# State visits of a hybrid decoder step: the outer product of dt·x and B made on VectorE from PSUM instead of on GpSimd from a copy

## The chip, the cores and the metric

One Trainium2 chip, one of its cores. The time is that of one launch of the whole program in device microseconds, the median of several runs. A profiled execution of the same program gives the span and the rows below.

## What is computed

One inference step of a layer with two branches, for a prompt of 512 tokens and a decode batch of 8 samples. The part that the change touches is the sample side of the state-space branch. For each of 8 samples b, 32 heads of 64 rows and 128 state columns:

```
h' = exp(dt*A) * h + (dt*x) outer B        # new state, an output
y  = C . h'                                # read of the state
```

The kernel treats the 32·64 = 2,048 rows as 16 units u of 128 partitions; a unit is a tile of 128 partitions x 8 samples x 128 columns (512 KB), loaded from the input and stored to the output. Four units share a group g of B and C. y is not read from the new state: the kernel forms C.h from the old state, scales it by the decay, and adds (dt*x)*(B.C) afterwards. So the new state is only stored, and the old one is read before it is overwritten.

## The kernel before

The kernel is written by hand for each engine. One list, PLAN, gives the order of steps; each engine walks it and issues its part of each step, so every engine's queue is in program order and semaphores join them. Projections are float32 products split in a high and a low part (three products each): each weight item is loaded by SyncE (`w_raw`), rounded to `wH` by ScalarE (L1136, a helper for all its copies) and its rest `wL` made by VectorE (L1511, both inputs in SBUF). TensorE takes PSUM banks 0 to 3 in turn for the projections and waits for VectorE's or ScalarE's `free` of the unit two before.

The 16 visits are laid beside 19 pieces of projection work, "beats" 0 to 18: three gs pieces (0 to 2), four ga (3 to 6), four ba (7 to 10), four ga (11 to 14), four ba (15 to 18). A gs or ga piece is 48 matmuls of 260 columns, a ba piece 24. In a beat the order is: the next item's `wH` and `wL` where one is due, TensorE's piece, at beats 4, 8 and 12 the spreads of a new group (`sgroup`), the visit (`sread`), ScalarE's decay of the visit before (`sdecay`), SyncE's load of a later unit into a freed slot (`sload`), and the use of the piece's result; a ba piece's use adds to `mix` on VectorE (L1622) and frees its two banks. From beat 14 on ScalarE and VectorE also split the prompt's y into `yH` and `yL` (L1925, both inputs in SBUF), four units a beat.

For a group, `sgroup` makes TensorE spread the samples' C row over all partitions into banks 4 and 5 and the B row into banks 6 and 7 (L920). ScalarE's `sbcopy` copies banks 6 and 7 to `Bsp` in SBUF and frees them at once. A visit is then:

- VectorE: `sc` = slot times the C spread in banks 4 and 5 (L1898, two halves), and a reduction of `sc` to y8 (L1905). After the fourth visit's `sc` it frees banks 4 and 5, ahead of the reduction.
- ScalarE: the decay of the slot, 8 instructions (L1429), once `sc` has been read.
- GpSimd: `outer` = Bsp times XD (dt·x) (L1116), then slot + outer (L1121), then the store's issue (L1123).

There are five slots; SyncE reloads one (L1001) once its store has landed, and its queue also holds the weight loads and the shifts of the key/value caches.

Of the kernel before, what the change touches and what calls it, by code (L numbers as in the profile page):

```python
# [21 lines left out]
ALU = mybir.AluOpType  # L22
ACT = mybir.ActivationFunctionType
AX = mybir.AxisListType

P = 128
D = 1024
T = 512
B = 8
# [7 lines left out]
UNITS = DSSD // P  # L37
PER_GROUP = UNITS // GROUPS
# [56 lines left out]
def plan():  # L95
# [128 lines left out]
    for beat, (kind, j, unit) in enumerate(rest):  # L224
        use = proj(kind, j, unit=unit)
        if beat < UNITS:
            if beat and beat % PER_GROUP == 0:
                out.append(("sgroup", beat // PER_GROUP))
            out.append(("sread", beat))
        if beat % PER_GROUP == 1 and beat < UNITS:  # L230
            out.append(("sbcopy", beat // PER_GROUP))
        if 0 < beat <= UNITS:
            out.append(("sdecay", beat - 1))
        if SLOTS_S <= beat - 2 < UNITS:
            out.append(("sload", beat - 2))
        if kind == "ba" and j == 1 and unit > 0:
            out.append(("sfinal", unit - 1))
        out.append(use)
        left = len(rest) - 1 - beat
        if left <= 4:  # L240
            out += [("parts", u) for u in range(4 * (4 - left), 4 * (5 - left)) if u < UNITS]
# [77 lines left out]
def hybrid_kernel(nc, xT, wpack, params, consts, sel_in, state_conv, ssm_in, caches,  # L319
                  y_out, tail_out, ssmp_out, kvp_out, ssms_out, kvs_out):  # L320
    ctx = ExitStack()
    with ctx:
# [3 lines left out]
        def sb(name, shape, dt=F32):  # L326
# [136 lines left out]
        Bsp = a4.tile("Bsp", [P, B, P])  # L463
        outer = a4.tile("outer", [P, B, P])
# [19 lines left out]
        names = """squares_added ac_parts_ready act_order b_rows_ready b_spread_ready b_spread_used bc_samples_kept cache_shifted cached_v_used  # L484
# [10 lines left out]
            sample_dt_ready sample_exponents sample_exps sample_probs sample_probs_turned  # L495
# [534 lines left out]
        def _(pool):  # L1030
            nbar = 0
            outs = 0
            for step in PLAN:
# [75 lines left out]
                elif op == "sread":  # L1109
# [3 lines left out]
                    pool.wait_ge(S["b_spread_ready"], 2 * (g + 1))  # L1113
                    if u == 0:
                        pool.wait_ge(S["sample_xdt_ready"], 1)
                    nc.gpsimd.tensor_tensor(outer[:, :, :], Bsp[:, :, :], XD[:, u, :].unsqueeze(2).to_broadcast([P, B, P]),  # L1116
                                            ALU.mult).then_inc(S["sample_outer_ready"], 1)
# [3 lines left out]
                    nc.gpsimd.tensor_tensor(st_u[:, :, :], st_u[:, :, :], outer[:, :, :], ALU.add).then_inc(S["sample_state_ready"], 1)  # L1121
# [8 lines left out]
        def _(act):  # L1130
# [4 lines left out]
            def cp(out, in_):  # L1135
                return nc.scalar.copy(out, in_)  # L1136

            def free(bk):
                act.sem_inc(bk.freed, 1)
# [10 lines left out]
            for step in PLAN:  # L1150
# [261 lines left out]
                elif op == "sbcopy":  # L1412

                    g = a[0]
                    if g > 0:
                        act.wait_ge(S["sample_outer_ready"], PER_GROUP * g)
                    for half in range(2):
                        bk = banks[6 + half]
                        bk.full(act, ("Bsp", g, half))
                        cp(Bsp[:, 4 * half:4 * half + 4, :], bk.tile[:, :].rearrange("p (c n) -> p c n", c=4)).then_inc(S["b_spread_ready"], 1)  # L1420
                        act.wait_ge(S["b_spread_ready"], 2 * g + half + 1)
                        free(bk)
# [25 lines left out]
        def _(dve):  # L1448
# [5 lines left out]
            def free(bk):  # L1454
                dve.sem_inc(bk.freed, 1)  # L1455
# [4 lines left out]
            for step in PLAN:  # L1460
# [428 lines left out]
                elif op == "sread":  # L1889
# [11 lines left out]
                    dve.wait_ge(S["sample_state_read"], u + 1)  # L1901
                    if u % PER_GROUP == PER_GROUP - 1:
                        free(banks[4])
                        free(banks[5])
                    ch.link(V.tensor_reduce(y8[:, u, :], sc[:, :, :], AX.X, ALU.add))  # L1905
# [138 lines left out]
```

## Time and profile before

| what | us |
|---|---|
| median of 3 runs | 1186.77 (1186.63 to 1190.5) |
| the profiled execution's own time | 1187.57 |
| its span | 1185.8 |

The profiled execution is 0.8 us above the median, and 1.8 us of its time lie outside the span. The visits run from about 917 us (first `sc`) to 1029 us (last store's issue) of the span; TensorE is busy almost throughout, with a few gaps that the rows below give, and from 1042 us it works on the last projections.

### The profile page before, as it was taken

The numbers are of one execution on the slowest core, as the hardware profiler recorded it, in microseconds if no ns is written. First come the engines' busy times: TensorE is split into PE (matmuls) and PEld (weight loads), VectorE is DVE, ScalarE is ACT, GpSimd is POOL, SyncE is SP. The second block draws the span as 40 slices with busy tenths as digits, with TensorE's granted clock in tenths as the row PEclk, the third lists the DMA queues.
The fourth block names the chain that finished last, engine by engine and source line by source line (L and its number), as shares of the span: only waits on it lengthen the run. The fifth ranks groups of instructions, "written<-read, shape, count | busy, mean of one in ns | idle before, by whom it ended". The sixth has DMA issues, their size and how long they took to land.

```text
span 1185.8 us, 19650 instructions
## 1 busy us (share of the span) xinstructions
PE 1097.8 (93%) x7838; PEld 1010.2 (85%) x7838; DVE 656.7 (55%) x936; ACT 499.4 (42%) x1130; POOL 219.8 (19%) x209
## 2 busy tenths in 40 slices
PE   4999989999999989895999999999998999689998
PEld 3887779977988779775999899898998999689998
DVE  6663527622462347237677677776764466834342
ACT  5334533345333544102554645656445566612210
POOL 0330003400231000000211220221120589500000
PEclk9998899989999899756999999999999999789999
DMA  8546102580242047145056246254446899432221
GB/s 348 213 169 276 55 1 116 213 329 1 107 168 81 1 151 246 58 152 232 1 219 235 109 162 254 110 218 163 182 175 273 343 360 343 155 144 80 100 98 46
DMA packets 29819, 198.14 MB, mean 167 GB/s; under 512 B 4104, under 2 KB 6280, under 8 KB 20224
## 3 DMA queue, kind: packets, MB, share of 16 engines
q1 hardware_dynamic: 25712, 183.35, 40.5%
q0 software_dynamic: 4016, 13.54, 3.0%
q8 instruction: 62, 1.02, 0.3%
q14 instruction: 29, 0.24, 0.1%
HBM read 180.16 MB, written 104.70 MB: 240 GB/s over the span
## 4 chain that ended last, share of the span: by engine, by line
PE 73%; DVE 11%; ACT 7%; issue 4%; DMA 2%; POOL 2%; SPq 0%; DVEq 0%; ACTq 0%; POOLq 0%
PE bank L618 36%; PE bank L590 16%; DVE cacc L1575 2%; PE bank L813 2%; PE bank L715 2%; ACT wH L1136 2%; PE bank L678 2%; PE bank L767 2%; POOL t L1080 2%; PE bank L884 1%; PE bank L654 1%; DVE wL L1511 1%; DMA slot<-in_state_ssm 1%; PE bank L902 1%; PE bank L876 1%
## 5 line engine op out<-in xcount | busy, mean ns | idle before, releaser
L1511 DVE TENSOR_TENSOR wL<-w_raw,wH 128x2048 fp32r<-128x2048 f32 (+1 forms) x63 | 145.0, 2302 | 155.0 <-ACT wH L1136 152.9
L618 PE MATMUL bank<-xH,wH 128*128 128x260 f32 x976 | 207.9, 294 | 8.1 <-DVEq L1455 6.9
L618 PE MATMUL bank<-xH,wL 128*128 128x260 f32 x976 | 198.1, 285 | 0.0
L618 PE MATMUL bank<-xL,wH 128*128 128x260 f32 x976 | 197.8, 284 | 0.0
L1136 ACT CAST wH<-w_raw 128x2048 fp32r<-128x2048 f32 (+1 forms) x63 | 119.2, 1892 | 136.2 <-PE bank L618 84.8
L618 PEld LDWEIGHTS bank<-xH,wH 128*128 128x128 f32 x976 | 152.0, 191 | 18.8 <-issue 16.6
L618 PEld LDWEIGHTS bank<-xH,wL 128*128 128x128 f32 x976 | 152.0, 190 | 0.0
L618 PEld LDWEIGHTS bank<-xL,wH 128*128 128x128 f32 x976 | 152.0, 190 | 0.0
L590 PE MATMUL bank<-wH,xH 128*128 128x512 f32 x336 | 136.7, 407 | 10.0 <-DVE xL L1490 6.0
L590 PE MATMUL bank<-wH,xL 128*128 128x512 f32 x336 | 134.6, 401 | 0.0
L590 PE MATMUL bank<-wL,xH 128*128 128x512 f32 x336 | 134.6, 401 | 0.0
L590 PEld LDWEIGHTS bank<-wH,xH 128*128 128x128 f32 x336 | 84.0, 250 | 21.2 <-issue 7.0
L1080 POOL TENSOR_TENSOR t<-qn,ropeB 128x256 f32<-128x256 f32 (+1 forms) x60 | 56.0, 951 | 246.4 <-DVE qn L1539 246.3
L590 PEld LDWEIGHTS bank<-wL,xH 128*128 128x128 f32 x336 | 84.1, 250 | 7.8
L590 PEld LDWEIGHTS bank<-wH,xL 128*128 128x128 f32 x336 | 84.3, 251 | 7.4
L1575 DVE SCALAR_TENSOR_TENSOR cacc<-buf,wcv,cacc 128x544 f32<-128x544 f32 x72 | 56.5, 784 | 17.3 <-ACT cacc L1251 15.1
L1294 ACT ACTIVATE Sx<-Sx,nm 128x128 f32<-128x128 f32 x96 | 37.6, 392 | 57.9 <-DVE nm L1669 57.8
L1381 ACT ACTIVATE Lb<-bank,nac 128x128 f32<-128x128 f32 x128 | 36.7, 369 | 47.1 <-PE bank L862 44.3
L1104 POOL TENSOR_TENSOR Eb<-Eb,CT 128x512 f32<-128x512 f32 x32 | 54.0, 1707 | 11.7 <-ACT Eb L1372 11.7
L618 PE MATMUL bank<-yH,wH 128*128 128x260 f32 x256 | 52.6, 287 | 3.5 <-DVE yL L1928 3.5
L618 PE MATMUL bank<-yL,wH 128*128 128x260 f32 x256 | 52.5, 287 | 0.0
L618 PE MATMUL bank<-yH,wL 128*128 128x260 f32 x256 | 52.2, 285 | 0.0
(285 smaller groups left out, 1916.9 us busy)
## 6 DMA issues: line engine op xcount, KB each, us to landing
w_raw<-in_weights SPq DMA_DIRECT2D x62, 1024.0 KB, 5.3
out_kvs<-in_cache SPq DMA_DIRECT2D x16, 2044.0 KB, 10.2
ring<-in_cache SPq DMA_DIRECT2D x48, 256.0 KB, 3.2
slot<-in_state_ssm SPq DMA_DIRECT2D x16, 512.0 KB, 5.9
out_ssm_s<-slot POOLq DMA_DIRECT2D x16, 512.0 KB, 6.0
out_kvs<-in_cache SPq DMA_DIRECT2D x8, 508.0 KB, 8.8
out_kvp<-st POOLq DMA_DIRECT2D x9, 256.0 KB, 2.3
out_kvp<-vv POOLq DMA_DIRECT2D x9, 256.0 KB, 4.6
```

Source lines behind the costliest of these rows:

```text
L590: mm = pe.matmul(bk.tile[:, :], a[:, kk, cols], wslot(b, i)[:, k, :], start=(kk == 0 and n == 0), stop=(kk == KD - 1 and n == 2))
L618: mm = pe.matmul(bk[hf].tile[:, 0:HALF], wslot(w, i)[:, k, s * P:(s + 1) * P], x[:, k, hf * HALF:(hf + 1) * HALF], start=(k == 0 and n == ...
L678: mm = pe.matmul(bk.tile[:, t * P:(t + 1) * P], qT[o:o + HD, hp, t * P:(t + 1) * P], kT[o:o + HD, hp, t * P:(t + 1) * P], start=True, stop ...
L715: mm = pe.matmul(out, vv[:, t, h * HD:(h + 1) * HD], PT[:, n % 2, t, :], start=(t == 0), stop=True, skip_group_check=True)
L767: mm = pe.matmul(banks[6].tile[:, c:c + B + 1:B], KT[:, n % 2, hp, :], qd[:, q0, :], start=True, stop=True, skip_group_check=True)
L1080: ins = nc.gpsimd.tensor_tensor(o[:, :, x, :], v[:, :, 1 - x, :], rb, ALU.mult)
L1104: nc.gpsimd.tensor_tensor(Eb[:, u % 2, e, :], Eb[:, u % 2, e, :], CT[:, 0:T], ALU.mult).then_inc(S["scaled_c_ready"], 1)
L1136: return nc.scalar.copy(out, in_)
L1294: ins = A(Sx[:, n % 2, t, :], Sx[:, n % 2, t, :], ACT.Exp, bias=nm[:, n % 2, t:t + 1], accum_out=lst[:, g, t, h:h + 1])
L1381: ins = A(Lb[:, e, c, :], banks[5 + e].tile[:, c * P:(c + 1) * P], ACT.Exp, bias=nac[:, c, n:n + 1])
L1511: TT(wL[:, i % 2, 0:k * n], raw[:, i % 2, 0:k * n], wH[:, i % 2, 0:k * n].bitcast(F32), ALU.subtract)\
L1575: ins = STT(out=cacc[:, :], in0=bb[:, w:w + CONV], scalar=wcv[:, cu, w:w + 1], in1=cacc[:, :], op0=ALU.mult, op1=ALU.add)
```

## The change

VectorE makes `outer` itself, straight from banks 6 and 7, between a visit's `sc` and its reduction. `outer` has two buffers in place of `Bsp` and one; ScalarE's copy and GpSimd's product are gone. VectorE waits, before it overwrites an `outer` buffer, for GpSimd's addition two visits before. All four spread banks are now freed at a group's fourth visit, after its reduction. `sample_xdt_ready` is still signalled; nobody waits for it.

```diff
-        if beat % PER_GROUP == 1 and beat < UNITS:
-            out.append(("sbcopy", beat // PER_GROUP))
...
-        Bsp = a4.tile("Bsp", [P, B, P])
-        outer = a4.tile("outer", [P, B, P])
+        outer = a4.tile("outer", [P, 2, B, P])
...
-                    pool.wait_ge(S["b_spread_ready"], 2 * (g + 1))
-                    if u == 0:
-                        pool.wait_ge(S["sample_xdt_ready"], 1)
-                    nc.gpsimd.tensor_tensor(outer[:, :, :], Bsp[:, :, :], XD[:, u, :].unsqueeze(2).to_broadcast([P, B, P]),
-                                            ALU.mult).then_inc(S["sample_outer_ready"], 1)
                     pool.wait_ge(S["sample_outer_ready"], u + 1)
                     pool.wait_ge(S["sample_decayed"], u + 1)
                     st_u = slots[u % SLOTS_S]
-                    nc.gpsimd.tensor_tensor(st_u[:, :, :], st_u[:, :, :], outer[:, :, :], ALU.add).then_inc(S["sample_state_ready"], 1)
+                    nc.gpsimd.tensor_tensor(st_u[:, :, :], st_u[:, :, :], outer[:, u % 2, :, :], ALU.add).then_inc(S["sample_state_ready"], 1)
...
-                elif op == "sbcopy":
-
-                    g = a[0]
-                    if g > 0:
-                        act.wait_ge(S["sample_outer_ready"], PER_GROUP * g)
-                    for half in range(2):
-                        bk = banks[6 + half]
-                        bk.full(act, ("Bsp", g, half))
-                        cp(Bsp[:, 4 * half:4 * half + 4, :], bk.tile[:, :].rearrange("p (c n) -> p c n", c=4)).then_inc(S["b_spread_ready"], 1)
-                        act.wait_ge(S["b_spread_ready"], 2 * g + half + 1)
-                        free(bk)
...
                     ins.then_inc(S["sample_state_read"], 1)
                     dve.wait_ge(S["sample_state_read"], u + 1)
+                    if u >= 2:
+                        dve.wait_ge(S["sample_state_ready"], u - 1)
+                    for half in range(2):
+                        bk = banks[6 + half]
+                        bk.full(dve, ("Bsp", g, half))
+                        ins = TT(outer[:, u % 2, 4 * half:4 * half + 4, :], bk.tile[:, :].rearrange("p (c n) -> p c n", c=4),
+                                 XD[:, u, 4 * half:4 * half + 4].unsqueeze(2).to_broadcast([P, 4, P]), ALU.mult)
+                    ins.then_inc(S["sample_outer_ready"], 1)
+                    ch.link(V.tensor_reduce(y8[:, u, :], sc[:, :, :], AX.X, ALU.add))
                     if u % PER_GROUP == PER_GROUP - 1:
-                        free(banks[4])
-                        free(banks[5])
-                    ch.link(V.tensor_reduce(y8[:, u, :], sc[:, :, :], AX.X, ALU.add))
+                        dve.wait_ge(S["sample_outer_ready"], u + 1)
+                        for bk in banks[4:8]:
+                            free(bk)
```

VectorE's queue at visit 7, the last of group 1, before (slot_158 is its slot, filled4 and filled5 are the C spread's banks):

```order
L1511 TENSOR_TENSOR wL<-w_raw,wH 128x2048 [waits s_weight_high_ready,s_dve_order]
L1898 TENSOR_TENSOR sc<-slot_158,bank 128x512 [waits filled4,s_state_loaded2]
L1898 TENSOR_TENSOR sc<-slot_158,bank 128x512 [waits filled5]
L1905 TENSOR_REDUCE y_164<-sc 128x8 [waits s_sample_state_read]
L1622 SCALAR_TENSOR_TENSOR mix<-mix,bank 128x260 [waits filled2,s_gate_ready,s_dve_order]
L1622 SCALAR_TENSOR_TENSOR mix<-mix,bank 128x260 [waits s_dve_order,filled3]
```

and the same place with the change (names and lines are numbered one or more lower there):

```order
L1492 TENSOR_TENSOR wL<-w_raw,wH 128x2048 [waits s_weight_high_ready,s_dve_order]
L1879 TENSOR_TENSOR sc<-slot_157,bank 128x512 [waits filled4,s_state_loaded2]
L1879 TENSOR_TENSOR sc<-slot_157,bank 128x512 [waits filled5]
L1888 TENSOR_TENSOR outer<-bank,XD 128x512 [waits filled6,s_sample_state_ready,s_sample_state_read]
L1888 TENSOR_TENSOR outer<-bank,XD 128x512 [waits filled7]
L1891 TENSOR_REDUCE y_163<-sc 128x8
L1603 SCALAR_TENSOR_TENSOR mix<-mix,bank 128x260 [waits s_dve_order,s_sample_outer_ready,filled2,s_gate_ready]
L1603 SCALAR_TENSOR_TENSOR mix<-mix,bank 128x260 [waits s_dve_order,filled3]
```

Two products stand between `sc` and the reduction, and the group's banks, freed before the reduction, are now freed behind it.

The other place is ScalarE's queue at the start of group 2, before:

```order
L1429 ACTIVATE slot_158<-slot_158,dsb 128x128 [waits s_sample_state_read]
L1429 ACTIVATE slot_158<-slot_158,dsb 128x128 x7
L1136 COPY Bsp<-bank 128x512 [waits filled6,s_sample_outer_ready]
L1136 COPY Bsp<-bank 128x512 [waits s_b_spread_ready,filled7]
L1429 ACTIVATE slot_159<-slot_159,dsb 128x128 [waits s_b_spread_ready,s_sample_state_read]
```

With the change the two copies are gone there, and the decay of visit 8 stands directly behind that of visit 7.

## Rows read from the trace of the kernel before

**Rows 1.** The page: engine, busy us, share of the span, instructions.
```profile
PE 1097.8 (93%) x7838; PEld 1010.2 (85%) x7838; DVE 656.7 (55%) x936; ACT 499.4 (42%) x1130; POOL 219.8 (19%) x209
```

**Rows 2.** Timeline of TensorE: start, us, what, [idle before, who ended it].
```profile
950.39 3.73 PE L920 MATMUL bank<-con,BCS 128*128 128x128 f32 x32
...
972.84 3.84 PE L920 MATMUL bank<-con,BCS 128*128 128x128 f32 x32 [1.44 <-DVEq L1455]
983.00 0.47 PE L618 MATMUL bank<-xH,wH 128*128 128x260 f32 x2 [0.57 <-DVEq L1455]
995.54 3.84 PE L920 MATMUL bank<-con,BCS 128*128 128x128 f32 x32 [0.81 <-DVEq L1455]
...
1024.83 0.77 PE L618 MATMUL bank<-oH,wH 128*128 128x260 f32 x2 [8.14 <-DVEq L1455]
```

**Rows 3.** The chain that ended last, 900 to 1060 us: start, us, what.
```profile
999.38 11.55 PE bank L618 x96
```

**Rows 4.** By tile: count, duration ns min/median/max, first and last start.
```profile
L1116 POOL TENSOR_TENSOR outer<-Bsp,XD x16: 1898/1905/3261, 932.0 to 1023.7; 128x1024 f32<-128x1024 f32 x16
L1121 POOL TENSOR_TENSOR slot<-slot,outer x16: 2352/2402/4332, 934.9 to 1025.7; 128x1024 f32<-128x1024 f32 x16
L1136 ACT COPY Bsp<-bank x8: 579/588/590, 930.5 to 1001.4; 128x512 f32<-128x512 f32 x8
L1898 DVE TENSOR_TENSOR sc<-slot,bank x32: 672/682/689, 917.6 to 1021.1; 128x512 f32<-128x512 f32 x32
```

**Rows 5.** Timeline of VectorE, visits 3 and 7 to 11.
```profile
944.64 1.27 DVE L1898 TENSOR_TENSOR sc<-slot,bank 128x512 f32<-128x512 f32 x2
...
968.88 2.65 DVE L1511 TENSOR_TENSOR wL<-w_raw,wH 128x2048 fp32r<-128x2048 f32 x1 [3.55 <-ACT wH L1136]
...
972.96 1.22 DVE L1905 TENSOR_REDUCE y<-sc 128x8 f32<-128x1024 f32 x1 [0.24 <-DVE sc L1898]
...
975.44 1.28 DVE L1898 TENSOR_TENSOR sc<-slot,bank 128x512 f32<-128x512 f32 x2 [0.22 <-DVE mix L1622]
...
979.23 1.29 DVE L1898 TENSOR_TENSOR sc<-slot,bank 128x512 f32<-128x512 f32 x2 [0.22 <-DVE mix L1622]
...
981.81 0.99 DVE L1622 SCALAR_TENSOR_TENSOR mix<-mix,bank 128x260 f32<-128x260 f32 x2
...
994.15 1.29 DVE L1898 TENSOR_TENSOR sc<-slot,bank 128x512 f32<-128x512 f32 x2 [4.83 <-DMA slot<-in_state_ssm]
```

**Rows 6.** Timeline of TensorE at the first spread.
```profile
915.03 0.64 PE L907 MATMUL bank<-cbp,ones 128*128 128x32 f32 x2 [3.26 <-DVE cbp L1884]
915.48 6.24 PE L920 MATMUL bank<-con,BCS 128*128 128x128 f32 x32
```

**Rows 7.** Windows: PE, PEld, DVE, ACT, POOL busy us; granted clock; DMA share, GB/s.
```profile
913.00:914.00 1.00, 0.00 (x0) 0.00 (x0) 1.00 (x1) 0.34 (x1) 0.00 (x0) 0.87 0.88 274
...
920.00:921.00 1.00, 1.00 (x9) 1.00 (x9) 1.00 (x1) 0.00 (x0) 0.00 (x0) 0.72 1.11 459
```

**Rows 8.** Timeline of VectorE, beats 14 to 17.
```profile
1013.19 5.19 DVE L1925 TENSOR_TENSOR yL<-ygn,yH 128x512 fp32r<-128x512 f32 x4 [2.48 <-ACT yH L1136]
...
1014.27 2.90 DVE L1925 TENSOR_TENSOR yL<-ygn,yH 128x512 fp32r<-128x512 f32 x1
...
1020.51 1.27 DVE L1898 TENSOR_TENSOR sc<-slot,bank 128x512 f32<-128x512 f32 x2
...
1024.77 5.40 DVE L1925 TENSOR_TENSOR yL<-ygn,yH 128x512 fp32r<-128x512 f32 x4
...
1033.38 2.50 DVE L1925 TENSOR_TENSOR yL<-ygn,yH 128x512 fp32r<-128x512 f32 x4
```

**Rows 9.** Timeline of GpSimd, visits 14 and 15.
```profile
1014.72 1.90 POOL L1116 TENSOR_TENSOR outer<-Bsp,XD 128x1024 f32<-128x1024 f32 x1
...
1025.69 2.72 POOL L1121 TENSOR_TENSOR slot<-slot,outer 128x1024 f32<-128x1024 f32 x1
```

**Rows 10.** Timeline of ScalarE, the last weight split beside the visits.
```profile
1014.56 1.91 ACT L1136 CAST wH<-w_raw 128x2048 fp32r<-128x2048 f32 x1
```

More of the change, by code:

```diff
@@ L482, in hybrid_kernel @@
                       sem(f"filled{i}"), sem(f"freed{i}")) for i in range(8)]
-        names = """squares_added ac_parts_ready act_order b_rows_ready b_spread_ready b_spread_used bc_samples_kept cache_shifted cached_v_used
+        names = """squares_added ac_parts_ready act_order b_rows_ready bc_samples_kept cache_shifted cached_v_used
             cb_products_ready chunk_decays_kept
@@ L494, in hybrid_kernel @@
             residual_loaded rope_sine_ready row_scale_ready rows_squared sample_decayed
-            sample_dt_ready sample_exponents sample_exps sample_probs sample_probs_turned
+            sample_exponents sample_exps sample_probs sample_probs_turned
             sample_q_ready sample_scores_kept sample_squares_ready sample_state_read
```

## The prediction

> **What bounds the kernel now.** I read the page first: TensorE is busy 93% of the span, VectorE 55%, GpSimd 19% [rows 1]. GpSimd is the engine that the change relieves, and it ends nothing in the TensorE timeline. So I went to TensorE's gaps in the stage of the visits. There are three small ones, 1.44 us ahead of the spread at beat 8, 0.57 ahead of beat 11 and 0.81 ahead of the spread at beat 12, and a large one, 8.14 us ahead of beat 17 [rows 2]. Each is ended by VectorE's `free` (L1455 is that helper). In between TensorE is full: two ga pieces of 48 matmuls take 11.55 us [rows 3], so a ga piece is 5.8 and a ba piece of 24 matmuls 2.9. The stage is therefore TensorE-bound up to beat 16 and bound by the work of VectorE (with ScalarE's copies ahead of it) from there to the start of the last projections. The change adds to the engine that ends every gap.
>
> **What it removes.** On GpSimd 16 products of 1.9 us; ScalarE's eight copies of 0.59 us [rows 4]. Neither stands ahead of TensorE's gaps, but for one thing: GpSimd's instructions hold up VectorE's where both of VectorE's inputs are in SBUF. The second `yL` took 2.90 us, with GpSimd's product of 1014.72 to 1016.62 inside it, and the four `yL` at 1024.77 took 5.40 us, with the addition of 1025.69 to 1028.41 inside, where four without GpSimd took 2.50 [rows 8, 9]. `sc`, one input of which is in PSUM, keeps to 672 to 689 ns in all 32 [rows 4], GpSimd busy or not. The Trainium skill ("SBUF — State Buffer", on the two separate sides) has it as a lock on a shared port pair, held for a whole instruction against a VectorE instruction with two SBUF inputs; the trace agrees (2.90 against 0.62). So products that leave GpSimd give time back to `yL` and `wL`, and the new ones, PSUM times XD, should not be held.
>
> **What it adds.** VectorE gets 32 products of 128x512, input in PSUM. No such row exists; the nearest is `sc`, same shape, one input in PSUM, a pair in 1.28 us [rows 4, 5]. Below, a pair can't well beat 1.22, the reduction of as many elements [rows 5]; above stands GpSimd's 1.9 [rows 4]. I take 1.28, and 1.32 with the 0.04 between instructions; 16 visits are 21 us of VectorE. The Trainium skill ("VectorE: DVE Perf Modes", rules for kernel authors) says of elementwise work on a matmul's result to accept the one-fold rate or copy it to SBUF first if many operations read it; four visits read these banks, so it speaks against the change. Here `sc` at 0.68 from PSUM stands beside `yL` at 0.62 from SBUF, which would be 0.06 an instruction, 2 us in all, of which less than one on the path.
>
> **Beat 8, the first spread that waits.** Before, `wL` starts at 968.88, tied to ScalarE's `wH` and so to TensorE, `sc` of visit 7 follows, and the free comes at 972.8 [rows 2, 5]. Now the free is behind two products and the reduction: `wL` of 2.65 us about 0.3 shorter (my estimate, as no product holds it), `sc` to 972.4, 0.24 of wait, product to 973.9, reduction to 975.1, TensorE at 975.3 instead of 972.84. That is +2.4, and the idle time grows from 1.4 to 3.9 us. At 1.4 the clock held. The nearest idle time to 3.9 is the 3.26 us before 915.03: the granted clock fell to 1.2 GHz within it (0.87 at 913) and was back in 920 to 921 (0.72), 5.4 us after the restart, so that the 32 spread matmuls took 6.24 in place of 3.84 us [rows 2, 6, 7]. I assume the same here: spread from 975.3 to 981.0, and VectorE, which needs each bank, reads the last B bank from about 981.4.
>
> **Beats 8 to 11, VectorE in step with ba pieces.** Before, a visit and its `mix` took 3.79 us (975.44 to 979.23 to the next) [rows 5] against 2.9 of TensorE. Now 5.11. Visit 8 ends its product at 982.1 and its reduction at 983.3, its `mix` and two frees last 1.2; visit 9 from 984.6, its `mix` at 988.5. TensorE's beat 11 needs the banks of beat 9: `mix` to restart was 981.81 to 983.00 [rows 2, 5], so 989.7 instead of 983.0. Beats 11 and 12 run to 1001.3. Visit 10 ends in a `mix` at 994.7; `wL` meets GpSimd's addition of visit 10 (about 993.6 to 996.0) and runs 996.0 to 998.3; visit 11, whose slot landed at about 994.1 before [rows 5], runs to 1002.3. TensorE starts its second spread at 1002.4, against 995.54: +6.9. If the clock doesn't fall, 2.8 us of this are gone and it is +4.1.
>
> **Beats 12 to 18.** TensorE carries +6.9 to the end of beat 14, after which ScalarE's `yH`, then four `yL`, `wL`, visit 15 and `mix` follow. Beat 14 ended at 1010.9 [rows 3], now 1017.8. Before, the `yL` started at 1013.19 and took 5.19 us, the lock included, and `wL` of 2.1 us ended where `sc` of visit 15 starts, at 1020.51; ScalarE's `wH` ended at 1016.5, 5.5 behind beat 14 [rows 8, 10]. Now VectorE comes out of visit 12 at 1008.2, out of `wL` at 1012.9 (held for 2.3 by the addition of visit 12), out of visits 13 and 14 at 1020.7. GpSimd's addition of visit 13 is over by then: `yL` to 1023.2, `wL` behind `wH` (1017.8 + 5.5) from 1023.4 to 1025.7, so +5.1. Visit 15 adds 1.32, so beat 17 starts at about 1031.2, +6.4. The last four `yL` start then too; the last addition, 1030.5 to 1032.9, holds the first of them for 1.7 us and they end at 1035.4, before 1030.2 [rows 8]: +5.2. From here to the last projections all is VectorE's own chain, and TensorE is full afterwards, so +5.2 stays. The sum: +2.4 (free behind product and reduction), +2.8 (clock), +1.7 (VectorE in step, the lock at `wL`), −1.8 (the lock gone from the `yL` of beat 14), +1.3 (visit 15), −1.2 (`yL` of beat 15). Against the profiled 1187.57 this is 1192.8; that execution is 0.8 above the median, so the median becomes **1192.0**.
>
> **What is hidden.** Groups 0 and 1: visit 3's free moves from 945.9 [rows 5] to about 948.7, and TensorE comes to that spread at 950.39, without idle time [rows 2]; visits 4 to 6 have VectorE time before the next `wL`. The new wait for GpSimd's addition two visits before is always over, since the addition lasts 2.4 us and a visit takes 3.9 or more. Stores start up to 3 us earlier where GpSimd was behind; loads follow, but the visit that mattered, 11, waited for the store of visit 6, which was tied to ScalarE's decay.
>
> **The rivals.**
> - *A, as above*, between +3.5 and +5.9: chance 0.40. The gap of 2.2 us ahead of beat 11 may drop the clock once more; that is hidden, since TensorE then waits less for visit 11's banks.
> - *B, the clock holds at beat 8*, or the additions miss `wL`: +4.1 at the second spread, then −1.8 +1.3 −1.2, so +2.4, 1189.2; with an earlier load of unit 11 some less. For it: idle times of 1.44 us did nothing. Against: 3.9 is longer than the 3.26 us that did. With everything from −1 to +3.5: 0.20.
> - *C, slower by more than 0.5%: the products are dear.* Place: visits 7 to 11 and 15, the six on the path. At GpSimd's 1.9 a pair costs 0.62 more each, +3.7, so 1195.7. It decides from (5.9 − 5.2) / 6 = 0.12 us, a pair at 1.40 or more. For it: the products wait for `sc` to be written (0.24 in [rows 5]) and read a second operand that repeats one element; against: `sc` never left 672 to 689 ns. With all else that ends above +5.9: 0.36.
> - *D, faster.* GpSimd was the pace of the stage by holding the slots: visit 11 waited 4.83 us for its slot [rows 5], and both locks vanish. If earlier stores brought all loads forward, the 0.81 goes, the `yL` give 2.7 + 2.9, and against them stand 1.3 of visit 15 and what is left of beat 8. It decides only if the VectorE pace at beats 8 to 11 is not what TensorE waits for, and 5.11 against 2.9 us speaks against that; 0.81 + 5.6 − 1.3 is −5.1 at best, 1181.7. Chance 0.04.
>
> **The numbers.** 0.5% of the time, 5.9 us, is about what a measurement of this kernel can tell from no change. A, B and D's weaker half lie within it: same 0.61, slower 0.36, faster 0.03. The range takes in B and most of C: 1188.5 to 1196.5.
>
> **What the profile will show.** Products of 0.68 us on VectorE and none on GpSimd; a gap of about 4 us ahead of the spread at beat 8, a granted clock of 0.5 through it and its 32 matmuls at about 6 us; 5.1 us from visit to visit in beats 8 to 10, a gap of about 2 us ahead of beat 11; `yL` of beat 14 in 2.5 us. Products well over 0.7, a slot that comes late for visits 12 to 15, or VectorE idle in beats 8 to 11 would make the prediction wrong.

## The result, and the profile after

The changed kernel takes 1189.78 us (median of 22 runs, 1187.54 to 1194.02), the kernel before 1186.84 us beside it: ratio 1.0029, 95% interval 1.0018 to 1.0040, which is +3.4 us; the two medians differ by 2.9. One execution each of the kernel before (1225.99 us), of e4 and of e8 took some 3% longer at a lower granted clock and is left out of the ratios. The forecast was 1192.0 with a range of 1188.5 to 1196.5 and within 0.5% as the likeliest. The profiled execution took 1192.29 us, its span is 1190.5.

The page of the changed kernel, busy time of each engine, beside [rows 1]:

```profile
PE 1102.2 (93%) x7838; PEld 1014.4 (85%) x7838; DVE 671.4 (56%) x968; ACT 493.1 (41%) x1122; POOL 183.8 (15%) x193
```

VectorE's busy time grew by 14.7 us, not by the 21.0 of its 32 products. Of the other 6.3 us, 4.1 is `yL`, which was held less, as its groups show, before and after (busy us, mean ns of one):

```profile
L1925 DVE TENSOR_TENSOR yL<-ygn,yH 128x512 fp32r<-128x512 f32 x16 | 15.6, 1035 | 2.9 <-ACT yH L1136 2.5
L1915 DVE TENSOR_TENSOR yL<-ygn,yH 128x512 fp32r<-128x512 f32 x16 | 11.5, 778 | 2.3 <-ACT yH L1128 1.9
```

`wL` gives 0.6 (143.8 to 143.2). Most of the rest is no saving: a product ends about 0.08 us after the reduction behind it has started, 16 times, and the page counts such a time once. The products themselves, by tile, beside [rows 4]:

```profile
L1888 DVE TENSOR_TENSOR outer<-bank,XD x32: 678/691/693, 922.1 to 1027.4; 128x512 f32<-128x512 f32 x32
L1879 DVE TENSOR_TENSOR sc<-slot,bank x32: 673/680/690, 918.7 to 1026.1; 128x512 f32<-128x512 f32 x32
L1113 POOL TENSOR_TENSOR slot<-slot,outer x16: 2339/2378/4371, 934.3 to 1030.2; 128x1024 f32<-128x1024 f32 x16
```

A product costs what a `sc` costs, and none is held. TensorE's timeline at the places of [rows 2]:

```profile
976.09 5.47 PE L917 MATMUL bank<-con,BCS 128*128 128x128 f32 x32 [3.56 <-DVEq L1436]
984.65 0.47 PE L615 MATMUL bank<-oH,wH 128*128 128x260 f32 x2 [0.21 <-DVEq L1436]
989.63 0.48 PE L615 MATMUL bank<-xH,wH 128*128 128x260 f32 x2 [1.86 <-DVEq L1436]
...
1030.95 0.77 PE L615 MATMUL bank<-oH,wH 128*128 128x260 f32 x2 [7.19 <-DVEq L1436]
```

The gap ahead of the second spread that waits (0.81 before) is gone, because TensorE itself comes to it late. VectorE's timeline at visits 7, 9, 10 and 11, at three `wL`, and at the two `yL` of beats 14 and 15, beside [rows 5, 8]:

```profile
970.02 2.29 DVE L1492 TENSOR_TENSOR wL<-w_raw,wH 128x2048 fp32r<-128x2048 f32 x1 [1.44 <-ACT wH L1128]
972.23 1.28 DVE L1879 TENSOR_TENSOR sc<-slot,bank 128x512 f32<-128x512 f32 x2
973.54 1.29 DVE L1888 TENSOR_TENSOR outer<-bank,XD 128x512 f32<-128x512 f32 x2
974.75 1.21 DVE L1891 TENSOR_REDUCE y<-sc 128x8 f32<-128x1024 f32 x1
...
984.66 1.28 DVE L1879 TENSOR_TENSOR sc<-slot,bank 128x512 f32<-128x512 f32 x2 [0.22 <-DVE mix L1603]
...
989.65 1.28 DVE L1879 TENSOR_TENSOR sc<-slot,bank 128x512 f32<-128x512 f32 x2 [0.22 <-DVE mix L1603]
...
994.56 3.54 DVE L1492 TENSOR_TENSOR wL<-w_raw,wH 128x2048 fp32r<-128x2048 f32 x1
...
1000.53 1.21 DVE L1891 TENSOR_REDUCE y<-sc 128x8 f32<-128x1024 f32 x1
...
1008.38 2.29 DVE L1492 TENSOR_TENSOR wL<-w_raw,wH 128x2048 fp32r<-128x2048 f32 x1
...
1019.98 2.50 DVE L1915 TENSOR_TENSOR yL<-ygn,yH 128x512 fp32r<-128x512 f32 x4 [1.91 <-ACT yH L1128]
...
1030.89 4.00 DVE L1915 TENSOR_TENSOR yL<-ygn,yH 128x512 fp32r<-128x512 f32 x4
```

The visit's own work is back to back, and from visit to visit it is 4.99 us. Against the beat of 2.9 us of TensorE that is the loss of beats 9 to 11. GpSimd's timeline shows the lock from both sides:

```profile
993.57 2.38 POOL L1113 TENSOR_TENSOR slot<-slot,outer 128x1024 f32<-128x1024 f32 x1 [1.74 <-ACT slot L1410]
...
1008.56 4.37 POOL L1113 TENSOR_TENSOR slot<-slot,outer 128x1024 f32<-128x1024 f32 x1 [3.40 <-ACT slot L1410]
```

The addition of 993.57 was first and the `wL` of 994.56 took 3.54 us; the `wL` of 1008.38 was first and the addition of 1008.56 took 4.37. Last, the windows of 1 us (columns as in [rows 7]) around the spread at beat 8, and behind the gap ahead of beat 11:

```profile
975.00:976.00 1.00, 0.00 (x0) 0.00 (x0) 0.95 (x1) 0.99 (x4) 0.57 (x1) 1.00 0.68 279
976.00:977.00 1.00, 0.91 (x5) 0.91 (x6) 0.42 (x1) 0.00 (x0) 0.86 (x1) 0.71 0.93 381
...
979.00:980.00 1.00, 1.00 (x7) 1.00 (x7) 0.36 (x1) 0.00 (x0) 0.35 (x1) 0.58 0.32 131
980.00:981.00 1.00, 1.00 (x11) 1.00 (x11) 0.52 (x2) 0.64 (x3) 0.00 (x0) 1.00 1.13 401
...
990.00:991.00 1.00, 1.00 (x7) 1.00 (x7) 0.97 (x3) 0.27 (x2) 0.96 (x1) 0.54 0.00 0
991.00:992.00 1.00, 1.00 (x7) 1.00 (x7) 1.00 (x2) 1.00 (x4) 0.57 (x1) 0.50 0.73 299
...
993.00:994.00 1.00, 1.00 (x9) 1.00 (x7) 0.82 (x3) 0.41 (x2) 0.43 (x1) 0.76 1.04 414
```

The clock (column ahead of the last two; 1.00 is 2.4 GHz, 0.50 is 1.2 GHz) is 1.00 to the end of the idle time. It falls to 1.2 GHz about 0.3 us after the spread has begun (a mean of 0.71 in 976 to 977) and is back at about 979.8: the 32 matmuls took 5.47 us. It fell once more from about 990.1 to 993.5, behind the gap of 1.86.

### The profile page after: what moved, and what is told of

Its sections match the earlier page's. It is cut to its first block, busy times and chain, and to the rows that moved or that the text cites. A ratio compares the mean times of both kernels' runs of the same rounds, so it can differ in the third digit from the quotient of the medians.

```text
span 1190.5 us, 19670 instructions
## 1 busy us (share of the span) xinstructions
PE 1102.2 (93%) x7838; PEld 1014.4 (85%) x7838; DVE 671.4 (56%) x968; ACT 493.1 (41%) x1122; POOL 183.8 (15%) x193
## 4 chain that ended last, share of the span: by engine, by line
PE 74%; DVE 11%; ACT 7%; issue 4%; POOL 2%; DMA 1%; SPq 0%; DVEq 0%; ACTq 0%
PE bank L615 37%; PE bank L587 16%; ACT wH L1128 2%; PE bank L712 2%; DVE cacc L1556 2%; PE bank L810 2%; PE bank L675 2%; PE bank L764 2%; POOL t L1077 2%; PE bank L917 2%; PE bank L881 1%; PE bank L651 1%; PE bank L899 1%; PE bank L873 1%; DVE wL L1492 1%
## 5 line engine op out<-in xcount | busy, mean ns | idle before, releaser
L1113 POOL TENSOR_TENSOR slot<-slot,outer 128x1024 f32<-128x1024 f32 x16 | 41.9, 2621 | 93.8 <-ACT slot L1410 93.8
```

## Where the time went, by landmarks

The stage starts between 912.1 and 919.5 us of the span from one execution to the next (e4 aside), for reasons ahead of it. So all kernels are read by four starts, in us after that execution's own `cbp` matmul, the first row of [rows 6]: the spreads of beats 8 and 12, beat 17, and the last projections. In brackets is the gap ahead, where there is one (not given for the last projections). The ratio is that of the timed runs, with its 95% interval, and is what counts; the landmarks are of one execution each and tell where.

| kernel | spread, beat 8 | spread, beat 12 | beat 17 | last projections | ratio |
|---|---|---|---|---|---|
| before | 57.81 (1.44) | 80.51 (0.81) | 109.80 (8.14) | 126.42 | 1 |
| after | 59.96 (3.56) | 86.62 | 114.82 (7.19) | 130.03 | 1.0029, 1.0018 to 1.0040 |
| e1 early free | 57.64 (1.08) | 83.38 | 111.70 (7.30) | 126.79 | 1.0021, 1.0003 to 1.0040 |
| e2 late free | 58.90 (2.34) | 82.87 (2.83) | 110.52 (6.55) | 127.22 | 0.9999, 0.9982 to 1.0016 |
| e3 groups 0 to 2 | 59.87 (3.56) | 86.54 | 113.59 (6.03) | 130.56 | 1.0040, 1.0023 to 1.0057 |
| e4 group 3 | 57.49 (1.08) | 82.69 (2.38) | 112.64 (7.19) | 127.86 | 0.9986, 0.9967 to 1.0005 |
| e5 twin on GpSimd | 57.78 (4.04) | 85.50 | 114.49 (7.98) | 130.40 | 1.0039, 1.0023 to 1.0056 |
| e6 use first | 61.37 (4.78) | 87.05 (1.66) | 115.37 (7.20) | 130.59 | 1.0015, 0.9999 to 1.0030 |
| e7 both repairs | 58.83 (2.31) | 80.97 (1.00) | 109.39 (7.31) | 124.49 | 0.9989, 0.9973 to 1.0006 |
| e8 group 3, last deferred | 57.46 (1.08) | 80.95 (1.41) | 107.85 (5.79) | 121.57 | 0.9956, 0.9939 to 0.9972 |
| e9 all, repaired, last deferred | 58.82 (2.31) | 81.02 (1.06) | 107.84 (5.71) | 121.57 | 0.9958, 0.9935 to 0.9982 |
| e10 group 3 again | 56.40 (1.09) | 79.74 (1.31) | 108.06 (7.20) | 123.31 | 0.9985, 0.9967 to 1.0003 |
| e11 GpSimd held | 56.41 (1.08) | 79.75 (1.15) | 108.61 (7.75) | 122.32 | 0.9970, 0.9957 to 0.9983 |
| e12 side edits | 56.80 (1.46) | 79.90 (1.16) | 108.80 (7.79) | 125.45 | 0.9993, 0.9975 to 1.0011 |

In e5, e10, e11 and e12 the first spread ran wholly or partly at full clock (see the end), so their landmarks are about 2.6, 1.1, 1.0 and 1.0 us earlier for that reason alone (by the start of the spread at beat 4, 35.36 in the kernel before and 32.73, 34.30, 34.32 and 34.33 in these). The stretches from landmark to landmark don't have this.

## The experiments

**e1, the banks freed as early as they can be.** The changed kernel with the frees of a group's last visit taken apart: the C banks behind `sc`, the B banks behind the products, the reduction last.

```diff
+                    if u % PER_GROUP == PER_GROUP - 1:
+                        free(banks[4])
+                        free(banks[5])
...
-                    ch.link(V.tensor_reduce(y8[:, u, :], sc[:, :, :], AX.X, ALU.add))
                     if u % PER_GROUP == PER_GROUP - 1:
                         dve.wait_ge(S["sample_outer_ready"], u + 1)
-                        for bk in banks[4:8]:
+                        for bk in banks[6:8]:
                             free(bk)
+                    ch.link(V.tensor_reduce(y8[:, u, :], sc[:, :, :], AX.X, ALU.add))
```

> The changed kernel, but each group's C banks are freed right behind the fourth visit's sc and its B banks right behind the products, ahead of the reduction. My theory: the spread at beat 8 then starts about 2.3 us sooner (gap ahead of it 1.3 us instead of 3.56), the granted clock stays at 1 through the spread (32 matmuls in 3.8 us instead of 5.5), and what is left of the loss is VectorE's pace of 5 us a visit in beats 8 to 10, about 1.5 to 2.5 us less than with the change as it is: +1 to +2 us against the kernel before (ratio 1.001). Rival P, only VectorE's total per visit counts and the place of the free does not: gap ahead of beat 11 grows by what the other gap loses, time as with the change, +3.4 us.

Measured: 1187.99 against 1186.13 us. TensorE's timeline around beat 8:

```profile
969.88 3.84 PE L917 MATMUL bank<-con,BCS 128*128 128x128 f32 x32 [1.08 <-DVEq L1436]
...
979.05 0.47 PE L615 MATMUL bank<-oH,wH 128*128 128x260 f32 x2 [1.88 <-DVEq L1436]
```

The gap of 3.56 is 1.08 and the spread 3.84 us. So the first term and the clock's fall at the spread both hang on where the frees stand. What is left at beat 12, +2.87, is VectorE in step with the ba pieces, of which the gap of 1.88, ahead of beat 10, is a part. Behind that gap the clock fell here too, as in the window of 980 to 981:

```profile
980.00:981.00 1.00, 1.00 (x6) 1.00 (x6) 0.97 (x3) 0.61 (x3) 0.70 (x2) 0.50 0.87 344
```

Even so the ratio is only 0.0008 below that of the full change, inside both intervals: the profile says −3.2 us at the last projections, the timed runs don't resolve it.

**e2, the late free alone.** The kernel before with `free(banks[4])` and `free(banks[5])` behind the reduction; GpSimd makes the products.

```diff
+                    ch.link(V.tensor_reduce(y8[:, u, :], sc[:, :, :], AX.X, ALU.add))
                     if u % PER_GROUP == PER_GROUP - 1:
                         free(banks[4])
                         free(banks[5])
-                    ch.link(V.tensor_reduce(y8[:, u, :], sc[:, :, :], AX.X, ALU.add))
```

> The kernel before, GpSimd making all products, but banks 4 and 5 are freed behind the reduction instead of ahead of it. My theory: the gap ahead of the spread at beat 8 grows from 1.4 to 2.7 us, the clock falls for some 3 us, TensorE is 1.5 us later at the second spread that waits, and +1.5 us reach the end (1.0013). Rival R, what is lost before beat 16 is taken up by the large gap ahead of beat 17: no difference.

TensorE's timeline at the spreads of beats 8 and 12:

```profile
971.14 3.84 PE L920 MATMUL bank<-con,BCS 128*128 128x128 f32 x32 [2.34 <-DVEq L1455]
...
995.11 3.84 PE L920 MATMUL bank<-con,BCS 128*128 128x128 f32 x32 [2.83 <-DVEq L1455]
```

and VectorE's at visit 11:

```profile
992.46 1.28 DVE L1898 TENSOR_TENSOR sc<-slot,bank 128x512 f32<-128x512 f32 x2 [5.89 <-DMA slot<-in_state_ssm]
```

At beat 8 the gap grows by 0.9 and the clock holds (32 matmuls in 3.84); its forecast fall didn't come. At beat 12 TensorE is 2.4 us later than before: the free is again behind the reduction (1.2), and visit 11's slot landed 1.1 us later than in the kernel before, for a reason that no run shows. The tail then gives 1.6 back (44.35 us from beat 12 to the last projections, 45.91 before), so these are 0.8 later and the ratio is 1. So the order free/reduction does cost TensorE time at both spreads, though without the clock's fall, and most of what it costs is taken up in the tail, as rival R had it.

**e3, groups 0 to 2 alone.** `VE` names the groups whose products VectorE makes, with `Bsp` as the second buffer; the last group goes the old way.

```diff
+VE = (0, 1, 2)
...
+                    if g in VE:
...
+                        for half in range(2):
+                            bk = banks[6 + half]
+                            bk.full(dve, ("Bsp", g, half))
+                            ins = TT(dst[:, 4 * half:4 * half + 4, :], bk.tile[:, :].rearrange("p (c n) -> p c n", c=4),
```

> Groups 0 to 2 as in the changed kernel (VectorE makes the products, banks freed behind the reduction), group 3 as before (ScalarE's copy, GpSimd's products). My theory: all of the loss up to the spread at beat 12 is there, +6 us as in the changed kernel, and none of what comes back in the tail, since GpSimd's products hold up yL again: +5 to +6.5 us at the end (1.005). Rival R, the loss is made in the tail by visit 15 and its neighbours and the early delay is absorbed: 0 to +1.

1190.77 against 1186.13 us. Everything up to beat 12 is as in the full change (86.54 against 86.62). VectorE's `yL` of beats 14 and 15:

```profile
1017.56 3.73 DVE L1946 TENSOR_TENSOR yL<-ygn,yH 128x512 fp32r<-128x512 f32 x4 [5.95 <-ACT yH L1139]
...
1027.32 5.76 DVE L1946 TENSOR_TENSOR yL<-ygn,yH 128x512 fp32r<-128x512 f32 x4
```

The second takes 5.76, as before. The first takes 3.73 although GpSimd makes these products, where the kernel before shows 5.19 and e2 3.53: how much of this `yL` is held depends on where GpSimd's work of visits 13 and 14 happens to lie. The forecast that nothing comes back in the tail was wrong: from the spread of beat 12 to the last projections it takes 44.02 us, 1.9 less than before (45.91), with the old way in group 3. So part of the tail's gain comes with TensorE's lateness alone.

**e4 and e10, group 3 alone.** `VE = (3,)`, from the kernel before; run twice, since the first profile has a span of 1224.7 us and can't be compared in its tail.

> Only group 3 as in the changed kernel, groups 0 to 2 as before. My theory: nothing is lost before beat 12; visit 15 costs 1.3 us, the four yL of beat 14 take 2.5 us instead of 5.2 and those of beat 15 lose about 1.3 us of lock: -1.5 to -2.7 us at the end (0.998), faster than both kernels. Rival R, the tail is where VectorE is short: +1.3 to +3.

> Group 3 alone on VectorE once more, since the profile of its first run fell in a disturbed execution. My theory: -1.5 to -2.7 us against the kernel before, the tail from the spread at beat 12 to the last projections about 43.5 us instead of 45.9. Rival: tail not shorter, 0 to +1.

Ratios 0.9986 and 0.9985, neither interval clear of 1. VectorE's `yL` in e10:

```profile
1016.04 2.50 DVE L1946 TENSOR_TENSOR yL<-ygn,yH 128x512 fp32r<-128x512 f32 x4 [0.29 <-ACT yH L1139]
...
1026.97 4.01 DVE L1946 TENSOR_TENSOR yL<-ygn,yH 128x512 fp32r<-128x512 f32 x4
```

From the spread of beat 12 to the last projections it takes 43.57 us where the kernel before takes 45.91: −2.3, as in the full change (43.41). With e3 the change is cut in two, groups 0 to 2 cost and group 3 gives, but the halves don't add up: +4.1 at the last projections in e3 and −2.0 in e10 (the shift of 1.1 taken out) make +2.1, and the full change has +3.6. Behind groups 0 to 2 the old group 3 gets 1.9 back by itself, so that moving it as well wins only 0.5 there, which the ratios of e3 and of the full change don't resolve.

**e5, a product on GpSimd as well.** The changed kernel in which GpSimd also multiplies `outer` by XD, in two halves, into a tile that nobody reads. It is work on top, of the size of the old product.

```diff
+                    for half in range(2):
+                        nc.gpsimd.tensor_tensor(junk[:, :, :], outer[:, u % 2, 4 * half:4 * half + 4, :],
+                                                XD[:, u, 4 * half:4 * half + 4].unsqueeze(2).to_broadcast([P, 4, P]), ALU.mult)\
+                            .then_inc(S["junk_made"], 1)
```

> The changed kernel, but GpSimd also makes a product of the same size from SBUF into a junk tile at each visit, ahead of its addition. It leaves out nothing and adds only this. My theory: TensorE reaches the second late spread (beat 12) as with the change, and the tail gets its holds back: the yL of beat 15 take about 5.4 us instead of 4.0, those of beat 14 up to 3.7 instead of 2.5, so +1.5 to +3 us against the change, +5 to +6.5 against the kernel before. Rival: what GpSimd does beside VectorE costs nothing in time at the end, +3.4 like the change.

1193.02 against 1188.1 us. VectorE's `yL`:

```profile
1016.71 4.19 DVE L1921 TENSOR_TENSOR yL<-ygn,yH 128x512 fp32r<-128x512 f32 x4 [1.90 <-ACT yH L1134]
...
1028.43 4.69 DVE L1921 TENSOR_TENSOR yL<-ygn,yH 128x512 fp32r<-128x512 f32 x4
```

Against 2.50 and 4.00: GpSimd's work holds them again, +2.4 us in the two rows, of which 1.5 reach the stretch from beat 12 to the last projections (44.90 against 43.41). The forecast that TensorE reaches beat 12 as with the change missed; GpSimd's twin also held the `wL` ahead of beat 8 (VectorE, then TensorE):

```profile
965.21 2.77 DVE L1498 TENSOR_TENSOR wL<-w_raw,wH 128x2048 fp32r<-128x2048 f32 x1 [1.17 <-ACT wH L1134]
```

```profile
971.77 6.53 PE L918 MATMUL bank<-con,BCS 128*128 128x128 f32 x32 [4.04 <-DVEq L1442]
```

The gap is 4.04, the clock stays down for the whole spread, and beat 12 comes 1.5 us later than in the full change (the shift of 2.6 taken out), so +3.0 at the last projections. In the ratio it is +0.0010 over the full change, within both intervals, so the size is shown in the profile alone.

**e6 and e7, the pace of beats 7 to 10.** e6 is the changed kernel with the use of a ba piece's result (the `mix` and its two frees) ahead of the visit in beats 7 to 10 (`j == 0`).

```diff
+            if kind == "ba" and j == 0:
+                out.append(use)
             out.append(("sread", beat))
...
-        out.append(use)
+        if not (kind == "ba" and j == 0):
+            out.append(use)
```

> The changed kernel, but in beats 7 to 10 every engine's use of the ba piece (VectorE's mix and its frees) stands ahead of the visit instead of behind it. My theory: the gaps ahead of beats 10 and 11 (0.21 and 1.86 us) and the second fall of the clock are gone, since the banks are freed 3.8 us sooner; the gap ahead of the spread at beat 8 stays (or grows by the 1.1 us of mix); the spread at beat 12 then waits for visit 11's free, so that only about 1 us is won against the change. Rival: the pace of VectorE in beats 8 to 10 was the whole loss, then 3 us are won and the time is that of the kernel before.

e7 is e6 with the frees of e1.

> The changed kernel with both repairs: use ahead of the visit in beats 7 to 10, and the spread banks freed right behind sc and behind the products. My theory: no gap but about 1 to 2 us at beat 8, none ahead of beats 10 and 11, the spread at beat 12 free when C is read: within 1.5 us of the kernel before at that spread, and with the shorter yL of beat 15 0 to -1.5 us at the end. Rival: VectorE is simply 21 us longer and it shows somewhere, +2 or more.

TensorE's timeline, e6 at the spread of beat 8:

```profile
973.61 6.72 PE L920 MATMUL bank<-con,BCS 128*128 128x128 f32 x32 [4.78 <-DVEq L1439]
```

and e7, the spreads of beats 8 and 12:

```profile
971.02 3.84 PE L920 MATMUL bank<-con,BCS 128*128 128x128 f32 x32 [2.31 <-DVEq L1439]
...
993.16 3.84 PE L920 MATMUL bank<-con,BCS 128*128 128x128 f32 x32 [1.00 <-DVEq L1439]
```

Alone, the repair of the pace moves the `mix` ahead of the free, so the gap at beat 8 grows to 4.78, the clock stays down for the whole spread (6.72), and nothing is won at beat 12. With both, beat 12 comes at 80.97, where the kernel before has 80.51: all but 0.5 of the +6.1 is accounted for by the place of the frees and the place of the `mix`, with all 32 products still on VectorE. The ratio of e7, 0.9989, doesn't tell it from the kernel before, and its interval is clear of the full change's (1.0018 and up).

**e8 and e9, the last product behind the chain.** e8 is e4 with the product of visit 15 issued behind the samples' `yL`, late in the tail. Two side edits go with it: the matmul of the samples' norm uses bank 4, and SyncE's load of the residual stands at mix 2, not mix 0. e9 is e7 with the same. The cut is from e9, whose `product` is a helper; in e8 the same lines are written out.

```diff
                     TT(yL[:, :, 0:B], ygn[:, :, 0:B], yH[:, :, 0:B].bitcast(F32), ALU.subtract).then_inc(S["sample_y_low_ready"], 1)
+                    product(UNITS - 1)
```

> Group 3 alone on VectorE, and the product of the last visit put behind VectorE's sample part of yL (after the last step that TensorE waits for); the group norm's sum uses bank 4 and the residual's load is issued two mix steps later, so that neither waits for it. My theory: TensorE's tail from the spread at beat 12 to the last projections, 45.9 us before and 43.4 with the change, is 1.3 us shorter still from the product and 1.4 from the last addition, which no longer holds a yL: about 40.8 to 42, the end at -3.5 to -5 us against the kernel before (0.9965). Rival: these us are taken by another wait in the tail (yH on ScalarE, mix), no gain over group 3 alone, -1.6.

> All products on VectorE as in the change, with use ahead of the visit in beats 7 to 10, the banks freed right behind their last reader, and the last visit's product behind VectorE's sample part of yL (group norm in bank 4, residual's load two mix steps later). My theory: the losses are places, not the amount of VectorE's work: the spread at beat 12 stands where it stood before within 1 us, the tail from there to the last projections takes about 40.6 us as with group 3 alone and the last product deferred; -4 to -5.5 us against the kernel before (0.996). Rival: the 15 us of products that VectorE has more than in that kernel before beat 12 cost something, -2 to -3.5.

1182.86 against 1188.1 us, and 1182.35 against 1188.25. VectorE's timeline of e8:

```profile
1013.66 2.50 DVE L1945 TENSOR_TENSOR yL<-ygn,yH 128x512 fp32r<-128x512 f32 x4
...
1022.70 2.50 DVE L1945 TENSOR_TENSOR yL<-ygn,yH 128x512 fp32r<-128x512 f32 x4
...
1036.25 1.28 DVE L1955 TENSOR_TENSOR outer<-bank,XD 128x512 f32<-128x512 f32 x2
1037.77 4.37 DVE L1516 TENSOR_TENSOR wL<-w_raw,wH 128x2048 fp32r<-128x2048 f32 x1 [0.24 <-DVE outer L1955]
```

Both `yL` take 2.50, and none of the 16 is held, as the view by tile shows:

```profile
L1945 DVE TENSOR_TENSOR yL<-ygn,yH x16: 683/684/694, 1013.7 to 1033.8; 128x512 fp32r<-128x512 f32 x16
```

From the spread of beat 12 to the last projections it is 40.62 us against 43.57 of e10, −2.95: 1.3 for the product that left the chain and 1.5 for the `yL` that GpSimd's addition of visit 15 no longer holds. The lock isn't gone: it now holds a `wL` (4.37) that TensorE doesn't wait for (from the last projections to the end of the span it is 143.3 us, 144.4 in the kernel before). e9 is its equal with four times as many products on VectorE.

**e11, GpSimd held back, no product moved.** The kernel before; GpSimd waits for the samples' `yL` ahead of visit 15's product and addition. With it goes the later load of the residual.

```diff
+                    if u == UNITS - 1:
+                        pool.wait_ge(S["sample_y_low_ready"], 1)
                     pool.wait_ge(S["b_spread_ready"], 2 * (g + 1))
```

> The kernel before, in which GpSimd's product and addition of visit 15 alone wait for VectorE's yL of the samples (after the four yL of the prompt's last units), and the residual's load stands at mix 2 in SyncE's queue instead of mix 0. No product moves to VectorE. Theory 'place, not engine': what the versions with the deferred last product won (0.9956) is that no GpSimd instruction of visit 15 stands beside the four yL of beat 15, so these take 2.5 us here in place of 5.40 of the kernel before, last projections 2.9 us earlier after the cbp matmul (about 123.5 in place of 126.4), ratio about 0.9975. Rival 'engine': the gain needs the products on VectorE, since GpSimd's product and addition together (4.3 us) now start at about 1041 and hold the wL at 1042 longer (4.4 or more in place of 2.3), so that TensorE waits at the last projections and the ratio is 1.000 or above. Rival 'load': the gain is that of the moved load, then e12 shows it too.

**e12, the side edits alone**, on the kernel before.

> The kernel before with only the two side edits of the deferred versions: the residual's load at mix 2 instead of mix 0, and the matmul of the samples' norm in bank 4 instead of 6. If these carried the gain of 0.9956, this kernel shows it: ratio under 0.998. If they are neutral, as I expect, the ratio is 1.000 within its interval, the four yL of beat 15 take 5.4 us and the last projections start 126.4 us after the cbp matmul.

e11: 1183.7 against 1187.1 us, ratio clear of 1. e12: 1187.02, no difference. VectorE's timeline of e11:

```profile
1012.71 4.81 DVE L1927 TENSOR_TENSOR yL<-ygn,yH 128x512 fp32r<-128x512 f32 x4 [2.88 <-ACT yH L1138]
...
1023.90 2.49 DVE L1927 TENSOR_TENSOR yL<-ygn,yH 128x512 fp32r<-128x512 f32 x4
...
1038.34 3.31 DVE L1513 TENSOR_TENSOR wL<-w_raw,wH 128x2048 fp32r<-128x2048 f32 x1 [0.82 <-ACT wH L1138]
```

The `yL` of beat 15 takes 2.49 in place of 5.40, from beat 17 to the last projections it is 13.71 in place of 16.62 us, and all of the 2.9 reaches the end. So the better part of what e8 and e9 win (4.9 us at the last projections in e8) has nothing to do with which engine makes the products: it is one wait that keeps GpSimd still while VectorE's chain reads two inputs from SBUF. The `yL` of beat 14 is still held here (4.81, in e8 2.50); that is the difference in the profile, 42.57 against 40.62 us behind the spread of beat 12. The ratios of e8 and e11 (0.9956 and 0.9970) overlap.

## Why the prediction was right

The likeliest case was taken, with its sign and its places; the sum came out at +5.2 and measured are +3.6 at the last projections, +3.4 by the ratio and +2.9 between the medians. The total is closer than its terms: two of them missed in opposite directions, and that is luck. By its own terms:

- **Price of a product**, 1.28 a pair: 1.29. Rival C, the dear product, falls with it. The forecast's 0.06 us in favour of SBUF was a misreading: it set one `sc` (0.68) beside a quarter of four overlapping `yL` (2.50). A single `yL` that GpSimd doesn't hold lasts as long as a product, as e8 shows, where none is held (684 ns against 691). The Trainium skill ("VectorE: DVE Perf Modes", rules for kernel authors) would have many operations on a matmul's result read a copy in SBUF. By these durations a copy would save nothing here; no run tries one. What speaks against reading from PSUM in this kernel isn't the rate but who holds the bank and for how long, as e1 shows.
- **+2.4, free behind product and reduction**: +2.15, gap 3.56 against the 3.9 forecast. The start of `wL` came as before, its hold by GpSimd was gone (2.29 against 2.65). e1 takes the term away by the order of the frees alone.
- **+2.8, the clock**: the spread took 1.6 longer, and this term was too dear. The forecast shows 1.9 of it (5.7 for 3.84) and doesn't work out the rest. The clock did fall, but only 0.3 us into the spread, not within the idle time as in [rows 7], and was back about 3.4 us later. e1, where it holds at this spread, saves only 0.9 from the spread of beat 8 to that of beat 12 (25.74 us against 26.66). So the term is 0.9 to 1.6. The rival B (it holds) would have been right for a gap of 2.3 (e2, e7, e9).
- **+1.7, VectorE in step, the lock at `wL`**: +2.3 by the remainder (6.1 − 2.15 − 1.6), +2.87 by e1; this term was too cheap. The pace was 4.99 for 5.11. The lock at the `wL` of beat 10 is there as forecast (3.54). The step that said that a second fall of the clock is hidden was wrong in part: visit 11 ended its reduction at 1001.74, TensorE started the spread at 1002.75 without idle time, so TensorE's slow start after the gap of 1.86 set it. A spread that waits starts about 0.1 us behind the reduction (975.96 and 976.09 at beat 8), so that is about 0.9 us.
- **−1.8, `yL` of beat 14**: its row is −2.7 (2.50 for 5.19), but VectorE first waited 1.91 for ScalarE's `yH`, and e3 has most of it (3.73) with GpSimd's products in place. From beat 12 to 17 the landmark moved by −1.1 together with **+1.3, visit 15**, so the term was −2.4 at the least in the profile; what of it is due to the products having left GpSimd isn't settled: by e3 and the full change it is 1.2 us (3.73 against 2.50), and the rest goes with TensorE's coming late.
- **−1.2, `yL` of beat 15**: −1.4 (4.00 for 5.40).
- **A hold of 2.3 at the `wL` of beat 12** was forecast and didn't come: `wL` was 0.18 us ahead of the addition and it was GpSimd that was held (4.37). It would have been hidden, as forecast.

Rival D, faster, held the right observation (the locks at `yL`, though in the changed kernel that of beat 15 was only shortened) and the wrong condition: the pace of visits had to be undone first. e7 did so and came level with the kernel before; e9, with the last product deferred, was faster. The predicted total was above the measured one by 1.6 us at the landmark, 0.8 before beat 12 and 0.8 behind it, and the predicted median, 1192.0, by 2.2. No run takes away ScalarE's eight copies alone, so their share isn't known. The rest of the profiled difference (span +4.7) is 1.1 us ahead of the stage, which isn't the change's.

## What to carry to other kernels

When work moves to the engine that frees the buffers, the order within that engine's turn can cost more than the work: here the products of visits 0 to 11 cost 0.5 us in all once the frees stood directly behind the last reader and the result's use ahead of the visit (e7). Only the product that stood in VectorE's own chain, that of visit 15, still cost its 1.3 us, until it was deferred (e8, e9). Before an engine is relieved of work, look whether holding it still at the right moment gives the same: one wait on GpSimd (e11) did better than the move. And judge a gap in TensorE's work by what its clock does behind it, as much as by its length.

## What the runs showed of the hardware

**The clock behind an idle time is not a function of its length.** TensorE stood still for the same 3.25 to 3.26 us ahead of the `cbp` matmul in several kernels. The clock had fallen to 1.2 GHz within it in the kernel before and after, and their spreads took 6.24 and 6.31 us; in e5 it didn't fall there at all, as the windows (columns as in [rows 7]) and TensorE's timeline show:

```profile
913.00:914.00 1.00, 0.01 (x1) 0.02 (x1) 1.00 (x3) 0.00 (x0) 0.00 (x0) 1.00 0.99 381
914.00:915.00 1.00, 1.00 (x9) 1.00 (x10) 0.32 (x2) 0.00 (x0) 0.00 (x0) 1.00 1.07 418
```

```profile
913.99 0.41 PE L905 MATMUL bank<-cbp,ones 128*128 128x32 f32 x2 [3.26 <-DVE cbp L1871]
914.23 3.82 PE L918 MATMUL bank<-con,BCS 128*128 128x128 f32 x32
```

Elsewhere it held behind 2.31 us (e7, e9) and behind 2.34 and 2.83 (e2), but fell for about 3.4 us behind 1.86 to 1.88 (the full change, e1, e3, e5) and behind 3.56. In e6 it fell within the gap of 4.78 and stayed down for nearly all of the spread. So a gap's price can only be given as a range from such rows: 0 to 2.9 us in a spread here.

**The lock between GpSimd and VectorE goes by who is first, with one exception.** Of two instructions that overlap, the later one is longer by about what is left of the earlier: `wL` 3.54 for 2.29 behind an addition that had 1.39 left, an addition 4.37 for 2.38 behind a `wL` that had 2.11 left. One row doesn't fit: the `yL` of 1014.27 in [rows 8] took 2.90 although the product of 1014.72 in [rows 9] is recorded behind it and took its usual 1.90. GpSimd's recorded spans are rough, and no run settles it. `sc` (673 to 690 ns) and the new products (678 to 693 ns), with one input in PSUM, were never held by GpSimd's additions. The Trainium skill ("SBUF — State Buffer", on the two separate sides) describes it as a lock for a whole instruction; the runs agree, and add that holding the GpSimd instruction back by a wait moves the price off the chain (e11: 5.40 to 2.49).
